# Sparse-attention heads in pairs on the lower and upper 64 rows of TensorE

## The reference

```python
s_c = jnp.einsum('bqhd,bnd->bhqn', qf, kc) * scale      # cmp: 15 compressed keys
s_s = jnp.einsum('bqhd,bqnkd->bhqnk', qf, ksg) * scale  # sel: chosen blocks of 64 (here all of the past)
s_w = jnp.einsum('bqhd,bkd->bhqk', qf, kwi) * scale     # win: window of 512 (here all of the past)
return gi[..., 0:1] * o_c + gi[..., 1:2] * o_s + gi[..., 2:3] * o_w
```

## Time and profile before

| | us |
|---|---|
| median of 3 runs | 1512.75 |
| range | 1512.39 to 1512.95 |
| profiled execution | 1513.02 |
| its span | 1511.3 |
| PE busy | 1486.2 |
| VectorE busy | 1213.0 |
| ScalarE busy | 999.9 |
| GpSimd busy | 82.7 |

### The profile page before, as it was taken

The page is one execution under the profiler, slowest core; times in us unless marked ns, Lnnn a source line. Parts: engine busy times, 40 slices in busy tenths (PEclk is TensorE's granted clock), DMA queues, the critical chain, the costliest instruction groups (busy, mean ns, idle before and its releaser), DMA issues.

```text
span 1511.3 us, 20046 instructions
## 1 busy us (share of the span) xinstructions
PE 1486.2 (98%) x7413; PEld 1245.9 (82%) x7413; DVE 1213.0 (80%) x1281; ACT 999.9 (66%) x892; POOL 82.7 (5%) x126
## 2 busy tenths in 40 slices
PE   8999999999999999999999999999999999999997
PEld 7987888887898888878888888888888888888885
DVE  7778545544677899999898899898988899889986
ACT  7476543343547577777787777777777777778765
POOL 3102000000000110000000000000000000000000
PEclk9999999999999999999999999999999999999999
DMA  9705655555530379999999999999999999999992
GB/s 322 245 2 144 233 175 192 190 195 165 187 121 2 112 268 396 396 344 393 396 343 395 394 359 381 395 389 350 395 394 345 394 396 343 395 396 344 393 396 84
DMA packets 189980, 444.23 MB, mean 294 GB/s; under 512 B 9729, under 2 KB 16014, under 8 KB 189918
## 3 DMA queue, kind: packets, MB, share of 16 engines
q1 hardware_dynamic: 185366, 427.81, 77.2%
q0 software_dynamic: 4528, 15.58, 3.8%
q10 hardware_dynamic: 24, 0.01, 0.0%
HBM read 435.51 MB, written 7.86 MB: 293 GB/s over the span
## 4 chain that ended last, share of the span: by engine, by line
PE 93%; DVE 3%; ACT 2%; issue 1%; POOL 0%; DMA 0%; SPq 0%; POOLq 0%; DVEq 0%; ACTq 0%
PE bank L476 27%; PE bank L477 26%; PE bank L475 26%; PE bank L616 3%; PE bank L536 2%; PE bank L730 1%; PE bank L619 1%; PE bank L778 1%; PE bank L747 1%; PE bank L788 0%; PE bank L1018 0%; DMA ring<-in_w_in_dram 0%; POOL rstd L1301 0%; PE bank L648 0%; DVE w_lo L1890 0%
## 5 line engine op out<-in xcount | busy, mean ns | idle before, releaser
L1890 DVE TENSOR_TENSOR w_lo<-ring,w_hi 128x2048 fp32r<-128x2048 f32 x372 | 846.6, 2291 | 176.8 <-ACT w_hi L1425 176.2
L1425 ACT ACTIVATE w_hi<-ring 128x2048 fp32r<-128x2048 f32 x372 | 712.1, 1917 | 223.2 <-PE bank L475 223.2
L476 PE MATMUL bank<-w_hi,xT_hi 128*128 128x512 f32 x896 | 354.0, 395 | 0.0
L477 PE MATMUL bank<-w_hi,xT_lo 128*128 128x512 f32 x896 | 349.9, 391 | 0.0
L475 PE MATMUL bank<-w_lo,xT_hi 128*128 128x512 f32 x896 | 240.2, 390 | 0.0
L476 PE MATMUL bank<-w_hi,hidT_hi 128*128 128x512 f32 x560 | 221.0, 395 | 2.8 <-DVE hidT_lo L1897 2.8
L477 PE MATMUL bank<-w_hi,hidT_lo 128*128 128x512 f32 x560 | 218.6, 390 | 0.0
L475 PEld LDWEIGHTS bank<-w_lo,xT_hi 128*128 128x128 f32 x896 | 168.4, 188 | 35.6
L477 PEld LDWEIGHTS bank<-w_hi,xT_lo 128*128 128x128 f32 x896 | 168.6, 188 | 33.6
L476 PEld LDWEIGHTS bank<-w_hi,xT_hi 128*128 128x128 f32 x896 | 168.5, 188 | 33.5
L476 PE MATMUL bank<-w_hi,hT_hi 128*128 128x512 f32 (+2 forms) x384 | 147.0, 386 | 5.1 <-DVE hT_lo L1845 2.7
(11 more groups left out here) (391 smaller groups left out, 1266.7 us busy)
## 6 DMA issues: line engine op xcount, KB each, us to landing
ring<-in_moe_w_gate_dram SPq DMA_DIRECT2D x112, 1024.0 KB, 9.5
ring<-in_moe_w_up_dram SPq DMA_DIRECT2D x112, 1024.0 KB, 9.3
ring<-in_moe_w_down_dram SPq DMA_DIRECT2D x112, 1024.0 KB, 9.1
ring<-in_ffn_w_gate_dram SPq DMA_DIRECT2D x14, 1024.0 KB, 5.1
ring<-in_ffn_w_up_dram SPq DMA_DIRECT2D x14, 1024.0 KB, 5.1
ring<-in_ffn_w_down_dram SPq DMA_DIRECT2D x14, 1024.0 KB, 4.9
ring<-in_w_in_dram SPq DMA_DIRECT2D x11, 1024.0 KB, 5.7
ring<-in_w_out_dram SPq DMA_DIRECT2D x8, 1024.0 KB, 8.9
```

Source lines behind the costliest of these rows:

```text
L476: pe.matmul(o, x_hi, w, start=start, stop=False)
L477: return pe.matmul(o, x_lo, w, start=False, stop=False)
L1425: act.activation(w_hi[:, (base + at) % SPLIT, :], ring[:, i, :], ACT.Copy).then_inc(hi_ready, 1)
L1890: dve.tensor_tensor(w_lo[:, v, :], ring[:, (base + at) % RING, :], w_hi[:, v, :].bitcast(F32), ALU.subtract).then_inc(lo_ready, 1)
```

## The change

Four things, in both layers. The queries of NSA are turned two heads at a time, 128 columns wide, into one bank, so that `nqT` has even heads on partitions 0 to 63 and odd heads on 64 to 127. The keys `kswT` and `kcT` are copied to partitions 64 to 127 by two DMAs from GpSimd's queue, on a new semaphore `keys_in`; the first sel job and the cmp jobs wait for it. Every score job but the first takes two banks at its start and fills them in turn: heads 0, 2 on one and 1, 3 on the other for sel, win and cmp (so lower and upper rows alternate with the banks), heads 0, 1 and 2, 3 for the second MLA job. The banks of a layer's score jobs become 15. The orders of the jobs and of all else stay.

```diff
-                at(b4, NH, S), take(2, S), take(NC), take(2 * HD), take(TB, SSD_H), take(4, HD),
+                at(b4, NH // 2, S), take(2, S), take(NC), take(2 * HD), take(TB, SSD_H), take(4, HD),
...
+        def heads_of(n):
+
+            br, tb = AJ[n]
+            if br == "mla":
+                return [[0, 1, 2, 3]] if tb == 0 else [[0, 1], [2, 3]]
+            return [[0, 2], [1, 3]]
...
                 pe.wait_ge(nsa_roped, l + 1)
+                b = bank(1)
                 for hp in range(2):
-                    b = bank(1)
-                    for i in range(2):
-                        c0 = O_NSA + (2 * hp + i) * HD
-                        for tb in range(TB):
-                            mm = pe.transpose(b[0:HD, (2 * i + tb) * P:(2 * i + tb + 1) * P],
-                                              utok[:, tb, c0:c0 + HD], ident[:, :])
-                    give(mm, 1)
+                    c0 = O_NSA + 2 * hp * HD
+                    for tb in range(TB):
+                        mm = pe.transpose(b[:, (2 * hp + tb) * P:(2 * hp + tb + 1) * P],
+                                          utok[:, tb, c0:c0 + 2 * HD], ident[:, :])
+                give(mm, 1)
...
                         pe.wait_ge(dve_took, mark["cmp", l])
-                    per = 4 if br == "cmp" else 512 // nk
-                    for g in range(4 // per):
-                        b = bank(0)
-                        if n == 7:
-                            keep_busy(b, 2)
-                        for i in range(per):
-                            h = g * per + i
-                            q, k = {"mla": (qT[0:QK, h, t0:t1], kT[0:QK, h, 0:nk]),
-                                    "cmp": (nqT[0:HD, h, t0:t1], kcT[0:HD, :]),
-                                    "sel": (nqT[0:HD, h, t0:t1], kswT[0:HD, 0, 0:nk]),
-                                    "win": (nqT[0:HD, h, t0:t1], kswT[0:HD, 1, 0:nk])}[br]
+                        pe.wait_ge(keys_in, 32 * (l + 1))
+                    elif br == "sel":
+                        pe.wait_ge(keys_in, 32 * l + 16)
+                    groups = heads_of(n)
+                    held = [bank(0) for _ in groups]
+                    if n == 7:
+                        keep_busy(held[0], 2)
+                    for i in range(len(groups[0])):
+                        for b, heads in zip(held, groups):
+                            h = heads[i]
+                            r = slice(h % 2 * HD, (h % 2 + 1) * HD)
+                            nq = nqT[r, h // 2, t0:t1]
+                            q, k = {"mla": (qT[0:QK, h, t0:t1], kT[0:QK, h, 0:nk]), "cmp": (nq, kcT[r, :]),
+                                    "sel": (nq, kswT[r, 0, 0:nk]), "win": (nq, kswT[r, 1, 0:nk])}[br]
                             mm = pe.matmul(b[:, i * nk:(i + 1) * nk], q, k, start=True, stop=True)
-                        give(mm, 0)
+                            if i == len(heads) - 1:
+                                give(mm, 0)
...
                 pool.memset(utok[:, :, KV0 + 4 * HD:KV0 + 4 * HD + 1], 1.0).then_inc(sum_cols, 1)
+                pool.wait_ge(act_took, mark["nsa", l])
+                pool.dma_start(kswT[HD:P, :, :], kswT[0:HD, :, :]).then_inc(keys_in, 16)
+                pool.wait_ge(dve_took, mark["cmp", l])
+                pool.dma_start(kcT[HD:P, :], kcT[0:HD, :]).then_inc(keys_in, 16)
                 roots(2, 0, False)
...
-                for hp in range(2):
-                    b = filled()
-                    act.activation(nqT[0:HD, 2 * hp:2 * hp + 2, :],
-                                   b[0:HD, :].rearrange("p (h t) -> p h t", h=2), ACT.Copy).then_inc(act_took, 1)
+                b = filled()
+                act.activation(nqT[:, :, :], b[:, :].rearrange("p (h t) -> p h t", h=2), ACT.Copy)\
+                    .then_inc(act_took, 1)
...
-                    for g in range(4 // per):
+                    for heads in heads_of(n):
                         b = filled()
-                        for i in range(per):
-                            h = g * per + i
+                        for i, h in enumerate(heads):
                             ins = dve.tensor_tensor_reduce(prob_of(n)[:, h, :], b[:, i * nk:(i + 1) * nk], m,
                                                            -scale, -NEG, ALU.add, ALU.min, rmin[:, n, h:h + 1])
```

More of the change, by code:

```diff
@@ L303, in trunk @@
         half_made, last_sums = sem("half_made"), sem("last_sums")
+        keys_in = sem("keys_in")
         cn_ready = sem("cn_ready")
@@ L1270, in _ @@
             for l in range(L):
+                (qtok, kcat, xb, xbc, qT, kT, nqT, kswT, kcT, ckv, nacs, cvals, cin, xtok, xdt, dec1, kvT2,
+                 dec0) = mix_bufs[l]
                 roots(1, 0, False)
```

## The result

The changed kernel takes 1515.38 us (median of 22 runs, 1513.75 to 1516.12), the kernel before in the same sets of runs 1512.82 (22 runs, 1512.39 to 1514.48). The ratio is 1.0014, 95% interval 1.0009 to 1.0020: slower by 2.6 us, less than the 3.0 us that the prediction called a change, and outside its range on the slow side (1514.4). It had said 1510.9.

What follows compares the result with a forecast made beforehand. TensorE (PE) bounds the kernel, 93% of the wait chain. Gains of 0.51 plus 0.44 for the transposes make 0.95 us a layer, 1.9 for both: profiled 1513.02 to 1511.1, median 0.27 lower, 1510.9 us; range 1509.4 to 1514.4.

Steps and rivals of the forecast that it cites:

- Part 1: Query transposes: eight of 64 columns become four of 128, saving 0.44 us a layer on PE's path.
- Part 5: Key copies from GpSimd's queue: 3 to 6 us each, needed 6.9 and 12 us after issue, so no wait.
- Part 3: Second MLA score job on two banks, only reordered: VectorE late by 0.25 to 0.3 us, done at 86.0.
- (a): products(0) before compress: its second bank waits for the second MLA bank until about 86.08; compress gains 0.30 us.
- Part 2: sel, win and cmp score blocks: 8 records fill 5 slots, saving 0.65 us at 256 columns, 0.33 in the others.
- rival 2: Score blocks, full stacking: a pair takes one head's time, four slots (1.06, 0.64, 0.55 us); 1510.2 us, chance 0.12.
- rival 3: Score blocks: each change between lower and upper rows costs 0.15 us, +0.44 a block; 1518.1 us, chance 0.10.
- Part 4: A layer's score blocks take 15 banks instead of 11, bringing bank waits before compress, in ssd_sums and before products(4).
- (b): ssd_sums: last-but-one bank waits for win scores, so 12 more records run behind the stall; products(2) at 102.62, 0.39 us late.
- the prediction's own sign of being wrong: No longer wait in ssd_sums, or last transpose (121.47) more than 1.3 or less than 0.5 us earlier a layer.

Runs made afterwards that it cites:

- e3: The changed kernel with heads 0, 2 (lower rows) then 1, 3 (upper rows), bank after bank instead of in turn: 1513.96 us.
- e7: The kernel before with scores on two banks in turn, no stacking, plus three filler products before the ssd_sums wait: 1514.91 us.
- e2: The kernel before with every score job but the first on two banks in turn, nothing stacked, no fillers: 1518.12 us.
- e1: The changed kernel with five filler products, result unused, put before PE's wait in ssd_sums: 1511.33 us.
- e4: The changed kernel with ssd_sums issued ahead of the win scores that held it up: 1512.38 us median, from 1510.38 to 1519.28.
- e6: e4 with ScalarE copying job 3's probabilities before job 4's exponentials, and products(0)'s bank taken behind compress: 1515.18 us median, 1508.14 to 1517.96.
- e5: e4 with three filler products before the wait ahead of products(3): 1510.45 us.
- e8: e6 with two filler products before the wait ahead of products(4): 1508.78 us.
- e9: e6 with ScalarE's copies also ahead of the exponentials for job 5, no fillers: 1507.00 us.

## Why the prediction was wrong

**Part 1 (transposes)** was right: 74.57 - 74.13 = 0.44 us for four wide ones, 0.87 for the eight. Part 5 was right too: no wait for the key copies. The times of parts 3 and 4 leave out the 0.44 of part 1, and the stretch started 0.27 later than before; so 0.17 has to be added to a time of the trace after to compare it with them. **Part 3** was right: VectorE is done with the second bank at 85.83, 86.00 in that count (86.0 foreseen). But PE goes on only 0.27 us later, at 86.10, where (a) had 0.08, so `compress` gained 0.11 us and not 0.30.

```profile
85.75 0.08 DVE L2127 DVE_READ_ACCUMULATOR2_ANT work<- 128x1 f32 x1
...
99.37 0.29 DVE L2127 CUSTOM_DVE_ANT_0 work<-bank,cbias 128x128 f32<-128x128 f32 x1 [0.67 <-ACT work L1583]
```

**Part 2 (stacking)** was mis-sized, on the good side. I had five slots, from the premise that records start in the order of issue. The blocks took 1.07, 0.64 and 0.55 us: four slots, as rival 2 had it (1.06, 0.64, 0.55). By e3 the premise itself is wrong: the lower rows' heads all come first there, and the block is as short. The Trainium skill, "TensorE: Matmul & The Clock Gate", Part 3, "The mechanism", says that a weight load is pulled ahead of running products when it goes to other rows; that agrees with the load-bound 15-column block, which halved. The same section says that products start strictly in order, and that isn't what e3's trace shows, where the record issued fourth starts in the last of the four pairs; here the measurement decides. There was no price for a change of rows (rival 3).

**Part 4 (banks)** was right in its waits: 2.3 us foreseen near 99.4 and 2.56 found from 97.4 to 99.94; 0.4 foreseen before products(4) and 0.50 found. VectorE started the win scores at 99.37, 99.54 in the prediction's count and 0.26 later than its 99.28, and PE went on 0.57 after that (0.56 foreseen). e7, and layer 0 of e2, confirm the size of the banks' lateness. **The step that failed is (b)**: "Then PE needs 1.44 (100.79 to 102.23) + 1.34. Products(2) start at 99.28 + 3.34 = 102.62." PE needed 2.48 + 1.93 and got to products(2) at 104.35. The durations were taken from rows in which PE came from a stall of 0.4 us; I priced the wait of 2.3 us as time lost once, and not as a change of the speed of what follows it; the prediction has no term for the clock at all. The term is 1.63 + 1.37 = 3.0 us in the profiled run, and by e1 against the changed kernel 4.05 us in the median. Without it the change takes 1511.33 us with fillers, which bring work of their own but fit in the idle time: 1.5 us under the kernel before by the medians, and 1513.02 - 1510.73 = 2.3 by the profiled executions, where 1.9 was forecast. By e1's stretches the gain is 0.99 and 0.98 us a layer, where 0.95 was forecast. That it comes out so close is in part luck: with four slots the prediction's own sum is 1.28 (rival 2), and VectorE's 0.26 took most of the difference back. The missing term is larger than all the gains together, and by it the prediction's own sign of being wrong came true: the last transpose had to come at least 0.5 us earlier a layer and came 0.65 later.

None of the rivals had this. The Trainium skill, "TensorE: Matmul & The Clock Gate", "Why this matters for your kernels", lists idle gaps between bursts of products as a cause of the drop to the lower clock; I weighed that page's rule on packing and not this one, though the prediction itself named the longest new idle stretch. The traces agree with the drop, here at a wait of 2.56 us and in other runs at shorter ones than that section of the Trainium skill warns of.

**What stays open** is what makes the clock fall. Of two waits of one length (e2, e4, e6) one was followed by the half clock and one not; in e6 it lasted 17 us where it was 3.4 elsewhere; and e2's run shows it again at 539.7 behind no long wait. The length of a wait alone doesn't decide: the kernel before has waits of 1.57 us (at 375.6) and 1.35 (at 150.2 and 390.1) in its feed-forward, as has every profiled run of this case, and the clock held behind each of them.

```profile
PE bank L476 <- DVE hidT_lo L1897: 2.8, 2, 1.6
```

What sets the stretch of the mixers apart is not shown. I have only profiles of one run each. What is shown is that with fillers in the wait (e1, e5, e7, e8) or without the wait (e9) no run's clock was below 0.998.

## What to carry to other kernels

A change that shortens the bound engine's work and gathers the rest of its idle time in one place can lose by it: add up a new wait twice, by its length and by what runs behind it if the clock falls to half; not every wait costs that, so give it a chance of its own. Read the granted clock in the stretch right after each wait that grows; when runs of one kernel spread, sort them by it before anything else. Then look first for an order that removes the wait (e9: copies that the next product needs go ahead of the next job's exponentials, 6.0 us under the kernel before), and fill it with idle products only where it can't be removed (e1, e8).

## What the runs showed of the hardware

- Idle stretches of PE of 2.56 us (both layers), 1.41 (e2, layer 1), 1.43 (e4, layer 1) and 1.23 (e6, layer 1) came before the half clock; 1.40 (e2), 1.44 (e4) and 1.23 (e6) in layer 0 did not, nor did 1.57, 1.35 and 1.18 in the feed-forward of any profiled run. Once (e2, at 539.7) the half clock came with no wait above 0.45 us in the 3.7 us before. It read 0.50 for some 3.4 us each time, in e6 for 17.
- Lower and upper rows run side by side whether the records come in turn or not: 1.07 us for eight 256-column records either way, 1.92 unstacked. The weight loads overlap too: 0.55 us for eight records of 15 columns against 0.99.
- Going over to another part of the array of the same tile size showed no cost: the blocks took no more than four records and the entry price, 4 x 0.216 + 0.19 = 1.05 against 1.07 us. What the 0.15 us read at L686 is the price of isn't shown.
- A copy of 128 KB inside the on-chip memory, from GpSimd's queue, took 2.3 us from issue to landing where no weights were streaming:

```profile
work<-work POOLq DMA_DIRECT2D x2, 128.0 KB, 2.3
```
